# The state-space branch in whole-prompt phases, norms and router by channel chunks, three combine banks: one rewrite of a hybrid layer's kernel

## What is computed

```python
proj = x @ w_in + b_in                      # 1024 -> 6 * 1024: bg, cg, xc, us, ga, gb
ya = (bg * short_conv(cg * xc)) @ w_conv_out
h_t = Lb * h_(t-1) + Bb us_t                # 64 groups x 64 complex states, diagonal
z = gelu(Re(C h_t) + d_skip * us)
yb = (z * sigmoid(z @ w_glu + b_glu)) @ w_ssm_out
m = sigmoid(ga) * ya + sigmoid(gb) * yb
x = layer_norm(ALPHA * x + m @ w_o)
f = routed(x) + shared(x)                   # 64 experts of width 256, top 8 by 4 of 8 groups
x = layer_norm(ALPHA * x + f)
```

## Time and profile before

| | |
|---|---|
| median of three runs | 1248.1 us (1247.64 to 1248.42) |
| span of the profiled execution, first to last instruction | 1232.5 us |
| PE, DVE, ACT, POOL busy | 1144.1, 455.5, 144.4, 117.1 us |
| mean granted clock of PE | 0.899 |
| HBM read | 268.15 MB |

### The profile page before, as it was taken

How to read it: one execution, slowest core, us unless ns; L and a number is a source line. 1 busy time by engine, 2 the same in 40 slices (tenths; PEclk the granted TensorE clock), 3 DMA queues, 4 the chain that set the end, 5 groups by cost and what they waited for, 6 DMA issues and landing times.

```text
span 1232.5 us, 14898 instructions
## 1 busy us (share of the span) xinstructions
PE 1144.1 (93%) x5550; PEld 678.8 (55%) x5550; DVE 455.5 (37%) x1044; ACT 144.4 (12%) x224; POOL 117.1 (9%) x79
## 2 busy tenths in 40 slices
PE   7999999999999999995799999999999999999983
PEld 6866666666666688884654444444444444444442
DVE  6845652463440521214533233223322332233235
ACT  1100000000000031000201111111111111111120
POOL 1023311331120000000000000000000000000000
PEclk9968766876777899996899999999999999999997
DMA  8311211111111056660239899999988998999900
GB/s 327 117 52 52 69 41 44 51 51 48 54 51 53 10 194 242 244 217 1 104 125 375 362 359 389 367 364 361 399 353 361 363 396 357 363 372 383 358 35 36
DMA packets 40292, 261.81 MB, mean 212 GB/s; under 512 B 9608, under 2 KB 10120, under 8 KB 23248
## 3 DMA queue, kind: packets, MB, share of 16 engines
q1 hardware_dynamic: 35376, 252.87, 52.1%
q0 software_dynamic: 4896, 8.66, 2.6%
HBM read 268.15 MB, written 2.53 MB: 220 GB/s over the span
## 4 chain that ended last, share of the span: by engine, by line
PE 53%; DVE 6%; ACT 4%; issue 1%; DVEq 0%; ACTq 0%
PE banks L1152 18%; PE banks L1057 10%; PE banks L1180 9%; PE banks L1140 9%; DVE proj L1014 4%; ACT ring L823 3%; PE banks L1111 2%; PE banks L1069 2%; PE banks L1095 1%; PE banks L1127 1%; ACT ring L836 1%; PE banks L1081 1%; DVE proj L902 0%; DVE us L890 0%; DVE proj L889 0%
## 5 line engine op out<-in xcount | busy, mean ns | idle before, releaser
L1014 DVE TENSOR_TENSOR proj<-proj,banks 128x264 f32<-128x264 f32 x264 | 113.2, 429 | 357.3 <-PE banks L1140 354.0
L1152 PE MATMUL banks<-gu,ring 128*64 128x512 f32 x1024 | 225.4, 592 | 1.3 <-ACT ring L823 1.3
L606 PE MATMUL banks<-xT,ring 128*128 128x264 f32 x512 | 211.5, 522 | 0.0
L1140 PE MATMUL banks<-us,ring 128*128 128x264 f32 x528 | 152.9, 412 | 8.7 <-ACT ring L840 1.2
L1152 PEld LDWEIGHTS banks<-gu,ring 128*64 128x64 f32 x1024 | 76.2, 137 | 144.4 <-issue 144.4
L1180 PE MATMUL banks<-dn,ring 128*64 128x512 f32 x512 | 116.9, 598 | 23.3 <-ACT ring L836 23.3
L545 PEld LDWEIGHTS banks<-seg_u,bT 32*128 32x128 f32 x576 | 96.8, 245 | 67.9 <-issue 67.9
L1140 PEld LDWEIGHTS banks<-us,ring 128*128 128x128 f32 x528 | 81.3, 188 | 93.5 <-DVE proj L1014 49.6
L545 PE MATMUL banks<-seg_u,bT 32*128 32x64 f32 x576 | 118.8, 349 | 0.0
L606 PEld LDWEIGHTS banks<-xT,ring 128*128 128x128 f32 x512 | 98.6, 229 | 23.5 <-issue 3.4
L776 POOL DMA_INDIRECT ring<-x_rows_dram,idx x34 | 36.0, 1059 | 590.6 <-DVE idx L989 590.6
(11 more groups left out here) (228 smaller groups left out, 944.1 us busy)
## 6 DMA issues: line engine op xcount, KB each, us to landing
gu<-w_gu SPq DMA_DIRECT2D x65, 2048.0 KB, 10.1
dn<-w_dn SPq DMA_DIRECT2D x65, 1024.0 KB, 6.6
ring<-w_front SPq DMA_DIRECT2D x80, 512.0 KB, 3.3
xT<-x_t SPq DMA_DIRECT2D x1, 1056.0 KB, 5.6
o_y<-proj SPq DMA_DIRECT2D x2, 528.0 KB, 2.7
hh<-b_sm SPq DMA_DIRECT2D x1, 1024.0 KB, 8.4
cS<-c_sm SPq DMA_DIRECT2D x1, 1024.0 KB, 10.4
x_rows_dram<-proj SPq DMA_DIRECT2D x2, 512.0 KB
```

Of the source, the lines that this page charges most:

```text
L606: ins = pe.matmul(psum[:, 5 + s % 2, 0:T], ring[:, slot, kc], xT[:, kc], start=(kc == 0), stop=(kc == KC - 1))
L1014: dve.tensor_tensor(acc[:, n], acc[:, n], psum[:, 4 + n % 2, 0:T], ALU.add).then_inc(added, 1)
L1140: pe.matmul(psum[:, 4 + n % 2, 0:T], y_rows[:, u, n * P:n * P + P], sw[:, u], start=True, stop=True).then_inc(combined, 1)
L1152: ins = pe.matmul(psum[SL * j:SL * j + SL, u, :], xg[:, u, k, SL * j:SL * j + SL], gu[:, 2 * u + j, k], start=(k == 0), stop=(k == KC - 1))
```

## The change

**State branch.** `ring` has 4 slots from the start. The segments are kept for scan and tables only. State inputs are made for all 264 tokens at once: after every second matmul of strips 11 to 18 two matmuls of 32 x 264 (`state_inputs`, L943), 64 in all, in place of 288 of 64 columns and 64 of 8. DVE turns them back from PSUM two tiles at a time (`turned_back`), POOL adds, then 8 scans over [128, 2112] run one after the other under the strips that follow, then the turning forward, with the last additions done by PE: `outputs(c)` has 8 matmuls of 264 and 8 of 256 columns behind strips 34, 35, 37, 38, 40, 41, 43 and 44. The skip term (`skip_added`) and the convolution run on DVE behind these, and the gates' sigmoids are done as the strips are emptied. The Sin of the angles comes before the first strip's emptying on ACT. The five stores of conv and scan states (8 to 256 KB) are issued among the strip loads on SP.

**Norms and router.** The sums of m @ w_o are taken one strip behind. The mean is subtracted per chunk on DVE, squares are made per chunk on ACT, and PE sums each as it comes. The router's weights are multiplied by the norm's gain on POOL, so that logits (L1022) need not wait for the normalised x; scores are turned back by three transposes. The group choice does all three token tiles in one operation each. The shared expert's four parts lie between the transposes, the counting and the selects.

**Expert loop.** One bank for gate and up, three (1, 4, 5) for `combine`. On PE the transposes of h come before those of the rows, on ACT likewise. SP issues both experts' `gu` at `gu_done`, then both `dn` at `dn_done`. The last combine is interleaved with the sums of the last norm, which ends chunk by chunk with four stores.

The diff, cut to its core (both sides shifted left):

```diff
-RING = 8
-PRE = KC + 4
+RING = 4
+UNIT = 2
+UNITS = NT // UNIT
+TURN_AT = 5
+X_FROM = CG + 3
+Y_AFTER = [34, 35, 37, 38, 40, 41, 43, 44]
...
-    def state_input(half, n):
-        c, i, r = n // (2 * PB), n // 2 % PB, n % 2
-        rows = slice(32 * i, 32 * i + 32)
-        ins = pe.matmul(bx[:, i, c, r, :], bT[rows, r, HC * half + c, :], seg_u[rows, HC * half + c, :], start=True, stop=True)
-        if n == 2 * HT - 1:
-            ins.then_inc(bx_ready, 1)
...
-for j in range(PER_HALF):
-    if j == 0:
-    for kc in range(KC):
-        ins = pe.matmul(psum[:, 5 + s % 2, 0:T], ring[:, slot, kc], xT[:, kc], start=(kc == 0), stop=(kc == KC - 1))
-        if kc == KC - 1:
-            ins.then_inc(strips_done, 1)
-        if j < 2:
-            for r in range(2):
-                state_input(1 - half, (j * KC + kc) * 2 + r)
-        elif j == 2:
-            for n in range(4):
-                output(1 - half, 2 * kc + n // 2, n % 2)
...
+def state_inputs(k, r):
+    c = UNIT * k // PB
+    if k % 2 == 0 and r == 0:
+        pe.wait_ge(bank_free[c % 2], c // 2 + 1)
+    if k:
+        pe.wait_ge(bx_used, 2 * (k - 1) + r + 1)
+    for j in range(UNIT):
+        i = (UNIT * k + j) % PB
+        rows = slice(32 * i, 32 * i + 32)
+        ins = pe.matmul(psum[:, 2 * r + j, 0:T], bT[rows, r, c, :], us[rows, c, :], start=True, stop=True)
+    ins.then_inc(bx_ready, 1)
...
+def outputs(c):
+    pe.wait_ge(rot_done, PB // UNIT * (c + 1))
+    if c > 1:
+        pe.wait_ge(y_used, c - 1)
+    for r in range(2):
+        for i in range(PB):
+            pe.matmul(y[32 * i:32 * i + 32], cS[:, r, PB * c + i], xt[:, r, :, PB * c + i], start=(r == 0), stop=False)
+    for r in range(2):
+        for i in range(PB):
+            ins = pe.matmul(y_prompt[32 * i:32 * i + 32], (c_re_neg, cS[:, 1])[r][:, PB * c + i], with_sine(c, i // UNIT, r)[:, :, i % UNIT],
+                            start=False, stop=(r == 1))
...
+    def inputs_between(k, n=n):
+        if k % 2:
+            half = (n - X_FROM) * 4 + k // 2
+            state_inputs(half // 2, half % 2)
+    strip(n, xT, between=inputs_between if X_FROM <= n < X_FROM + KC else None)
+    if n in Y_AFTER:
+        outputs(Y_AFTER.index(n))
...
+        x_in = by_segments(psum[:, 2 * r:2 * r + UNIT, 0:LP])
+        with_cos, with_sin = ((0, 3), (2, 1))[r]
+        dve.wait_ge(bx_ready, 2 * k + r + 1)
+        dve.tensor_tensor(half_prod(k, with_cos), x_in, ct, ALU.mult)
+        last = dve.tensor_tensor(half_prod(k, with_sin), x_in, sn, ALU.mult)
+        if r == 1:
+            last.then_inc(demod_done, 1)
...
+    for r in range(2):
+        seg = xt[:, r, s].rearrange("p t c -> p (t c)")
+        st.did(dve.tensor_tensor_scan(seg, decay.rearrange("p t c -> p (t c)"), seg, 0.0, ALU.mult, ALU.add))
...
-    do(dve.tensor_scalar(mu[:, 0], psum[:, 4, 0:T], 1.0 / D, None, ALU.mult))
-    do(dve.tensor_tensor(src, src, wide, ALU.subtract))
-    do(dve.tensor_tensor(sq[:], src, src, ALU.mult))
+    for n in range(KC):
+        dve.scalar_tensor_tensor(src[:, n], psum[:, MEAN_BANK[nth], 0:T], -1.0 / D, src[:, n], ALU.mult, ALU.add).then_inc(centered, 1)
+    for n in range(KC):
+        act.wait_ge(centered, nth * KC + n + 1)
+        act.activation(sq[:, n], src[:, n], ACT.Square).then_inc(squared, 1)
...
+SUM_BANKS = (1, 4, 5)
-    if n > 1:
-        pe.wait_ge(added, first + n)
-    pe.matmul(psum[:, 4 + n % 2, 0:T], y_rows[:, u, n * P:n * P + P], sw[:, u], start=True, stop=True).then_inc(combined, 1)
+    if n > 2:
+        pe.wait_ge(added, first + (n - 1))
+    pe.matmul(psum[:, SUM_BANKS[n % 3], 0:T], y_rows[:, u, n * P:n * P + P], sw[:, u], start=True, stop=True).then_inc(combined, 1)
...
+    pe.wait_ge(hx_ready, it + 2)
+    for f in range(FC):
+        ins = pe.transpose(psum[:, 7, f * P:f * P + P], h_sl[:, f * P:f * P + P], ident[:])
+    ins.then_inc(h_turned, 1)
     pe.wait_ge(gathered[1 - u], q * 16 + 16 * (u + 1))
     turn(1 - u)
     pe.wait_ge(select_ready, it + 3)
     pe.wait_ge(idx_ready, it + 2)
     select(u, (it + 2) % PAIRS)
-    pe.wait_ge(hx_ready, it + 2)
-    for f in range(FC):
-        ins = pe.transpose(psum[:, 7, f * P:f * P + P], h_sl[:, f * P:f * P + P], ident[:])
-    ins.then_inc(h_turned, 1)
...
-for s in range(SLOTS):
-    e = (q * SLOTS + s) % E
-    sp.wait_ge(gu_done, q * 2 + (s // 2 - 1))
-    sp.dma_start(gu[:, s], w_gu[bass.ds(e, 1)].rearrange("o p f -> (o p) f")).then_inc(gu_in[s], 16)
-    sp.wait_ge(dn_done, q * 2 + (s // 2 - 1))
-    sp.dma_start(dn[:, s], w_dn[bass.ds(e, 1)].rearrange("o p f -> (o p) f")).then_inc(dn_in[s], 16)
+sp.wait_ge(gu_done, q * 2 + (pair - 1))
+for s in (2 * pair, 2 * pair + 1):
+    e = (q * SLOTS + s) % E
+    sp.dma_start(gu[:, s], w_gu[bass.ds(e, 1)].rearrange("o p f -> (o p) f")).then_inc(gu_in[s], 16)
```

More of the change, by code:

```diff
@@ new lines, in norm @@
+                    do(dve.tensor_tensor(mu[:, 2], mu[:, 2], mu[:, 1], ALU.mult))
+                    do(dve.scalar_tensor_tensor(mu[:, 0], mu[:, 2], 1.5, mu[:, 1], ALU.add, ALU.mult))
+                biased, masked, left, picked, wts = (rt[:, i] for i in range(5))
+                gs, rank, cnt = (group[:, i] for i in range(3))
+                total, cm, over = small[:, 30:33], small[:, 33:34], small[:, 34:38]
+                dve.memset(scores_t, 0.5).then_inc(scores_cleared, 1)
+                dve.wait_ge(iotas_ready, 2)
@@ L949, in _ @@
                 dve.sem_inc(picks_ready, 1)
+                st.did(dve.tensor_scalar(left, pk, -1000.0, 1000.0, ALU.mult, ALU.add))
                 do(dve.tensor_tensor(wts, scores, picked, ALU.mult))
@@ L1089, in _ @@
                     ins.then_inc(xrow_turned, 1)
[L1091 to L1096 removed]
+                shared_in(1)
                 pe.wait_ge(picks_ready, 1)
```

1239 lines of the change are left out of this document (590 added, 649 removed).

## The result

The changed kernel takes 929.55 us (928.09 to 931.42, four runs); the kernel before, in the runs beside it, 1247.87 us (1246.73 to 1248.42). The ratio is 0.7451, with a 95% interval of 0.7419 to 0.7484.

The account below looks back on a forecast made before the run. TensorE was taken as the bound, busy nearly everywhere but at a lowered clock in the front end. Front end 229, strips 48 to 79 118, middle 47, loop 523, tail 26: span 943; plus 15.6, 959; said 962 us, range 938 to 1018.

Parts of the forecast that it names:

- With the 15.6 us that the runs are longer than this profile's span: Whole run: 15.6 us added to the predicted span of 943 us, giving 959 us.
- stalls that I did not find: Whole run: such stalls held likelier than gains, so the forecast was raised from 959 to 962 us.
- Expert loop, 16.35 us a step: 32 expert steps: 16.35 us each instead of 17.75, from shorter combine and no h wait; 523 us against 568.5.
- To strip 11: Start of the front end: first strips at 3.56 us each and 16 transposes of some 2 us, ending at 49.5 us.
- Strips 11 to 18: Front end: 28.5 us of strip work plus 32 input pairs at 0.95 us, 59 us, ending at 108.5.
- Strips 19 to 47: Front end: 103 us of strips and 17 us of output blocks, 120 us with DVE's 107 us under it.
- Norm, router, shared expert: Between strips and expert loop: 47 us (43 to 54) against 76.6, with picks at 24 us.
- The rule weighed: Strips 11 to 18: DVE multiplications with one PSUM input pass POOL freely; if they waited, 988 us.
- Clock in strips 11 to 18: Rival, 30 in 100: granted clock falls in strips 11 to 18; 1005 us, or 985 if it falls midway.
- Loop bound by DMA: Rival, 15 in 100: weight loads hold expert steps at 17.75 us, the loop gives nothing; 1007 us.
- DVE and POOL in turns: Rival, 7 in 100: DVE and POOL take turns in strips 11 to 18; 988 us.
- slower than before: Rival, 2 in 100: TensorE stays at 1.2 GHz in the expert loop; all 32 steps slow give 1410 us.

Follow-up runs that it names:

- the last two runs: Changed kernel, input pairs after every strip matmul, a quarter of the turning back: with 64 columns, 927.93 us; then both matmuls on the same rows and bank, 956.11 us.
- the repeated kernel before: The kernel before, unchanged, profiled and timed again: 1248.31, 1220.77, 1235.20 and 1237.31 us.

## Why the prediction was wrong, point by point

The direction was right and each stage but the loop came out within 4 us; the total was 32 us high, and most of that from two terms. That the front end came out only 2.5 us off is in part luck, since two of its errors cancel (+1.8 us up to strip 11, -3.8 in strips 11 to 18).

**"With the 15.6 us that the runs are longer than this profile's span"** is the step that failed. I took the difference between the median of some runs and the span of one other execution as a cost of each launch. A run is 1.8 us over its own span in the changed kernel (930.48 and 928.7) and about 2 us in the kernel before. The 15.6 us were a front end that had spent less time at the lower clock in the profiled execution; as that front end goes, so do they. That is 13.8 us of the miss; with 1.8 in place of 15.6 the same sum gives 948, inside the range. The 3 us that I added for **stalls that I did not find** were not there either.

**Expert loop, 16.35 us a step** measured 15.99, over 32 steps 11.2 us with its borders. Both parts were mis-sized. Combine: I let DVE's eight adds and the h product hold TensorE for 3.95 us. It went on after 3.79, at 611.26 us, while DVE's last adds ran until 611.89: the third bank lets TensorE leave combine before DVE does. The text's bracket had it (15.9 if unhindered). h: the 0.65 that I took off was less than the wait of 0.73 in the earlier trace rows, and the order gives 0.86.

**To strip 11**, 49.5: strip 11 began at 51.3. The 16 transposes took 1.7 us, but the first five strips took 20.2 us from 7.84, not 17.8. I took 3.56 us for a strip from the first one on; up to some 12.3 us the records are as long as at 0.50 (above), and half of those 4.5 us is 2.2 of the 2.4 us. DVE was no hindrance.

**Strips 11 to 18**, 59 us: 32 x 1.73 = 55.4. The pair costs 0.84, not 0.95. With 64 columns on two row groups it costs 0.56, so 200 more columns in both matmuls cost 0.28 us, less than the 0.34 that 200 columns of one take: the two run side by side. **The clock** stayed at 1.00. I chose that for a mixture "like neither" without knowing what had brought it down, so that it came true was luck. By the last two runs it was the pairs that run one after the other, and the changed kernel has none in these strips.

**Strips 19 to 47**, 120 us: 120.0. An output block took 1.9 us, not 2.1. Eight scans took 41.0 us (110.49 to 151.44), as predicted, and DVE was ahead of each block: TensorE never idled. w_conv_out at 226.5 for 229.

**Strips 48 to 79**, 118: 116.6. **Norm, router, shared expert**, 47: 49.5; the count of picks came at 369.20, 26 us after the last strip where I had 24, with TensorE idle for 1.46 us before the squares' sums and for 2.23 us behind the logits. **Tail**, 26: 24.2.

Summed: front -2.5, strips -1.4, middle +2.5, loop -11.2, tail -1.8 are, but for rounding, the 14.3 us from 943 to 928.7; with 13.8 and 3 they are 31.1 of the 32.4. The rest is the median, 0.9 us below the profiled run, and the rounding of 961.6 to 962.

**The rule weighed.** DVE's multiplications with an input in PSUM passed POOL freely. All 32 of L620 took 680 to 693 ns, while POOL was busy in 38 of the 55 us; two of them, at 84.15 and 85.81 us, began inside adds of POOL that ran from 83.72 and 84.94 and took 1.27 us each, as the others did.

**The rivals.** Clock in strips 11 to 18: did not happen, but was near. A wait for the pair before, of half a microsecond, did it (+46), and so did the denser mixture with the pause of 1.11 us that it brought (+32). The rival's price was 23 to 43 us, and its sum is wrong: twice the 59 us is 962 + 59 = 1021, not 1005. Loop bound by DMA: did not happen. The queues gave 411 GB/s over the steps and could give 424, so the 372 GB/s of the old step was what TensorE asked for, not a limit. DVE and POOL in turns, and slower than before: no sign.

**What stays open.** Why the lower level of the first strips ended at 10.7 us in one execution and at 12.3 in another. What holds the clock at 0.50 once it has fallen: in the run with added waits the last is that of 0.93 us before 64.67, and 0.50 lasts until the plain strips begin at 150 us. Whether the rows or the bank of the pair matter. And of the 221 us between the front ends of the repeated kernel before and of the changed one, the input matmuls account for 152.6 in the run without them; how the rest divides between the outputs, the single tokens' part and the waits was not tried.

## What to carry to other kernels

Read each run's time beside its own span before adding a difference between the two; where the spans of one kernel scatter, look for the stage whose granted clock does. Where small matmuls stand between large ones, try them in pairs on different row groups and banks: here it shortened the pair from 0.78 to 0.56 us at the same columns, and it kept the clock at 1.00. Watch for short waits in such a stretch, for here they brought the clock down too. And cost a wait from both of its ends: a bank more and two transposes moved were worth 0.91 and 0.86 us in each of 32 steps, and the two together needed nothing else of the rewrite.
